# Decay matrices of a state-space scan: running sums spread by transfers instead of matmuls, work of each group's rounds moved

## The reference

```
cs[l]      = sum over k <= l of (-dt[k] * exp(a))            # the running sum of the decay
L[m, l]    = exp(cs[l] - cs[m])  if m <= l, else 0           # the decay matrix of one head
y[l]       = sum over m of (C[l] . B[m]) * L[m, l] * dt[m] * x[m]   # inside the chunk
state      = sum over m of B[m] * dt[m] * exp(cs[127] - cs[m]) * x[m]
y[l]      += exp(cs[l]) * C[l] . state                       # second chunk only
```

## Time and profile before

| | |
|---|---|
| median of three runs | 3062.14 us (3058.6 to 3064.3) |
| profiled execution | 3059.77 us, its span 3057.9 us |
| PE busy | 2883.9 us, 94% of the span |
| DVE, ACT, POOL busy | 1018.7, 566.3, 204.0 us |
| mean granted TensorE clock | 0.981 |
| traffic | 703.97 MB, 230 GB/s on the mean |
| scan of layer 0 (groups) | about 270 to 408 us |
| scan of layer 1 (groups) | about 980 to 1118 us |

### The profile page before, as it was taken

The page is one execution under the profiler, slowest core; times in us unless marked ns, Lnnn a source line. Parts: engine busy times, 40 slices in busy tenths (PEclk is TensorE's granted clock), DMA queues, the critical chain, the costliest instruction groups (busy, mean ns, idle before and its releaser), DMA issues. The chain is left out here.

```text
span 3057.9 us, 34707 instructions
## 1 busy us (share of the span) xinstructions
PE 2883.9 (94%) x14328; PEld 1697.8 (56%) x14328; DVE 1018.7 (33%) x2615; ACT 566.3 (19%) x1308; POOL 204.0 (7%) x319
## 2 busy tenths in 40 slices
PE   7999999999999999999999999999978989988986
PEld 4576646864567655884556555444444455443432
DVE  3543533421544442541435432222223064211112
ACT  1321411100231321211145110000011051000001
POOL 0000041000000000000000010000012020000001
PEclk9999999999999999999999999999989999999998
DMA  5346437454246445543040379999994125999996
GB/s 208 138 157 245 170 123 250 138 175 145 85 145 248 168 139 201 207 157 106 22 152 8 140 287 426 428 427 426 427 355 126 58 88 221 427 426 426 427 427 280
DMA packets 181448, 703.97 MB, mean 230 GB/s; under 512 B 18042, under 2 KB 27322, under 8 KB 156192
## 3 DMA queue, kind: packets, MB, share of 16 engines
q1 hardware_dynamic: 163600, 667.51, 55.9%
q0 software_dynamic: 17392, 34.11, 3.5%
q10 hardware_dynamic: 288, 0.01, 0.0%
HBM read 694.09 MB, written 20.06 MB: 234 GB/s over the span
## 5 line engine op out<-in xcount | busy, mean ns | idle before, releaser
L566 PE MATMUL bank<-h1T,wslot 128*128 128x256 f32 x2176 | 473.7, 380 | 2.2 <-issue 2.1
L566 PEld LDWEIGHTS bank<-h1T,wslot 128*128 128x128 f32 x2176 | 412.1, 190 | 61.3 <-issue 5.9
L2551 PE MATMUL bank<-wslot,xgT 128*64 128x512 f32 x736 | 337.2, 614 | 36.5 <-DMA wslot<-in_moe_w_up 18.9
L2552 PE MATMUL bank<-wslot,xgT 128*64 128x512 f32 x752 | 340.2, 608 | 0.0
L2568 DVE TENSOR_TENSOR hid<-gs,bank 64x512 f32<-64x512 f32 x65 | 68.2, 1049 | 479.8 <-ACT gs L2562 479.8
L2551 PEld LDWEIGHTS bank<-wslot,xgT 128*64 128x64 f32 x736 | 100.9, 141 | 197.1 <-issue 197.1
L2526 PEld LDWEIGHTS bank<-sel,hT 128*128 128x128 f32 x1600 | 182.8, 193 | 30.4 <-issue 25.2
L2526 PE MATMUL bank<-sel,hT 128*128 128x128 f32 x1600 | 189.0, 279 | 4.4 <-DVE sel L2505 4.4
L2606 PE MATMUL bank<-wslot,aT 128*64 128x512 f32 x736 | 164.2, 595 | 0.6 <-DVE aT L667 0.6
L2562 ACT ACTIVATE gs<-bank 64x512 f32<-64x512 f32 x65 | 38.5, 592 | 494.4 <-PE bank L2552 494.4
L451 PE MATMUL bank<-wslot,h1T 128*128 128x512 f32 (+1 forms) x320 | 121.9, 536 | 4.2 <-DVE h1T L1919 4.2
(11 more groups left out here) (415 smaller groups left out, 3882.8 us busy)
## 6 DMA issues: line engine op xcount, KB each, us to landing
wslot<-in_moe_w_up SPq DMA_DIRECT2D x47, 2048.0 KB, 20.2
wslot<-in_moe_w_gate SPq DMA_DIRECT2D x46, 2048.0 KB, 22.9
wslot<-in_moe_w_down SPq DMA_DIRECT2D x46, 2048.0 KB, 23.2
wslot<-in_w_in SPq DMA_DIRECT2D x36, 2048.0 KB, 9.0
wslot<-in_w_ada SPq DMA_DIRECT2D x24, 2048.0 KB, 8.0
wslot<-in_ffn_w_up SPq DMA_DIRECT2D x20, 2048.0 KB, 9.0
another<-in_moe_w_up SPq DMA_DIRECT2D x10, 2048.0 KB, 17.5
late<-in_moe_w_gate SPq DMA_DIRECT2D x10, 2048.0 KB, 23.1
```

The source lines that it names most:

```text
L566: ins = pe.matmul(b.t[:, 0:width], w[:, k, j * P:(j + 1) * P], xT(k), start=(k == 0), stop=(k == kc - 1))
L2551: pe.matmul(bk.t[other, :], xt.t[:, k, mine], wg[:, k, :], start=(k == 0), stop=(k == KD - 1))
L2552: ins = pe.matmul(bk.t[mine, :], xt.t[:, k, mine], wu[:, k, :], start=(k == 0), stop=(k == KD - 1))
```

## The change

The running sums of each chunk, as rows (head by token), are now made by one more matmul in `sums`, copied to SBUF and stored to DRAM. Each decay buffer is then filled by one transfer of POOL that reads the rows of 8 heads and writes them to all 128 partitions (512 KB). Four such transfers are issued when `first_ssd` begins; each of the other four of a layer when line 1535 of a chunk is emitted. The 128 matmuls of line 1495 are gone; the mask is added in place, by the same DVE instruction with SBUF as its source. Products of keys and queries, mask and Exp move from round 3 to the end of round 1; xdec is made before xs and xdt. The tile `blank` goes, its memsets use a free tile, and ACT and DVE wait for the two stores from it after the feed-forward network of layer 0.

```
+class StepSums:
+    def __init__(self, K, ctx):
+        self.K, self.n = K, 0
+        self.rows = K.sb("sumrows", [SHEADS, TT, P], ctx=ctx)
+        self.kept = self.stored = []
+    def begin(self):
+        self.dram = self.K.nc.dram_tensor(f"sum_rows{self.n}", [TT, SHEADS, P], F32).ap()
+        self.n += 1
+        self.stored = []
+    def spread(self, chunks, turn):
+        self.chunks, self.turn, self.filled = iter(chunks), turn, {}
+        for _ in turn.bufs:
+            self.fill()
+    def fill(self):
+        at = next(self.chunks, None)
+        if at is None:
+            return
+        (g, t), dc = at, self.turn.next()
+        @self.K.block.gpsimd
+        def _(p):
+            self.filled[at] = dc, self.K.move(p, dc.t[:, :, :], self.dram[t, HPG * g:HPG * (g + 1), :].partition_broadcast(P),
+                                              *dc.free, *self.stored)
...
@@ step_sizes, sums @@
             pe.matmul(b.t[:, 0:SHEADS], K.c("upto"), d(ADT), start=True, stop=True)
+            pe.matmul(b.t[0:SHEADS, P:2 * P], d(ADT), K.c("upto"), start=True, stop=True)
             K.mp = K.pe.mark(pe.matmul(b.t[:, 64:64 + SHEADS], K.c("ones"), d(ADT), start=True, stop=True).then_inc(K.pe.sem, 1))
...
+            for due in K.due(v, *S.kept):
+                v.wait_ge(*due)
+            K.mc = K.dve.mark(v.tensor_copy(S.rows[:, t, :], b.t[0:SHEADS, P:2 * P]).then_inc(K.dve.sem, 1))
+        b.free = [K.mc]
+        @K.block.gpsimd
+        def _(g):
+            S.stored.append(K.move(g, S.dram[t], S.rows[:, t, :], K.mc))
+        S.kept = S.stored
...
@@ first_ssd @@
+        S.spread([(g, t) for g in range(GROUPS) for t in range(TT)], decay)
...
+        def decays(g, t):
+            dc, came = S.filled[g, t]
+            exps = []
+            for q in range(HPG // 4):
+                @block.vector
+                def _(v):
+                    for due in K.due(v, came):
+                        v.wait_ge(*due)
+                    K.mv = K.dve.mark(v.tensor_tensor(
+                        dc.t[:, 4 * q:4 * q + 4, :], dc.t[:, 4 * q:4 * q + 4, :],
+                        K.c("segmask").unsqueeze(1).broadcast_to([P, 4, P]), ALU.add).then_inc(K.dve.sem, 1))
+                @block.scalar
+                def _(act):
+                    for due in K.due(act, K.mv, *small):
+                        act.wait_ge(*due)
+                    for i in range(4):
+                        h = HPG * g + 4 * q + i
+                        K.ml = K.act.mark(act.activation(dc.t[:, 4 * q + i, :], dc.t[:, 4 * q + i, :], ACT.Exp,
+                                                         bias=dts[:, t, NCS, h:h + 1]).then_inc(K.act.sem, 1))
+                exps.append(K.ml)
+            return dc, exps
...
                 def use(bank, mk):
+                    if t == 0:
+                        @block.vector
+                        def _(v):
+                            for due in K.due(v, mk, *small, *prev):
+                                v.wait_ge(*due)
+                            K.mv = K.dve.mark(v.tensor_tensor(hv(xdec[:, :]), hv(bank[:, :]), per_head(t, W2), ALU.mult).then_inc(K.dve.sem, 1))
+                        xm["dec"] = K.mv
...
-                    if t == 0:
-                        @block.vector
-                        def _(v):
-                            K.mv = K.dve.mark(v.tensor_tensor(hv(xdec[:, :]), hv(bank[:, :]), per_head(t, W2), ALU.mult).then_inc(K.dve.sem, 1))
-                        xm["dec"] = K.mv
                     return K.mv
                 K.transposed([xbcT[:, ch, t * P:(t + 1) * P] for ch in chs], use, *[convd[c] for c in chs], *prev)
+            multiplied = []
+            for t in range(TT):
+                b, tl = K.banks.next(), slice(t * P, (t + 1) * P)
+                @block.tensor
+                def _(pe):
+                    for due in K.due(pe, convd[16 + g], convd[20 + g], *b.free):
+                        pe.wait_ge(*due)
+                    K.mp = K.pe.mark(pe.matmul(b.t[:, 0:P], BT[:, tl], CT[:, tl], start=True, stop=True).then_inc(K.pe.sem, 1))
+                multiplied.append(K.copy(0, cbT[:, t, :], b.t[:, 0:P], K.mp, *prev))
+                b.free = [multiplied[t]]
+            grown = [decays(g, t) for t in range(TT)]
             yield
...
             def chunk(t):
                 tl = slice(t * P, (t + 1) * P)
...
-                            ins = pe.matmul(bq.t[:, i * P:(i + 1) * P],
-                                            dts[:, t, ADT, h:h + 1].broadcast_to([P, P]), K.c("upto"),
-                                            start=True, stop=True)
...
-                        K.mv = K.dve.mark(v.tensor_tensor(
-                            dc.t[:, 4 * q:4 * q + 4, :], bq.t[:, :].rearrange("p (h l) -> p h l", h=4),
-                            K.c("segmask").unsqueeze(1).broadcast_to([P, 4, P]), ALU.add).then_inc(K.dve.sem, 1))
...
+                cm = multiplied[t]
+                dc, exps = grown[t]
                 yield
...
                 dc.free = [K.mp]
+                S.fill()
...
@@ first_block, end of layer 0 @@
+            if l == 0:
+                @block.scalar
+                def _(act):
+                    for due in K.due(act, *K.blanked):
+                        act.wait_ge(*due)
+                @block.vector
+                def _(v):
+                    for due in K.due(v, *K.blanked):
+                        v.wait_ge(*due)
...
```

More of the change, by code:

```diff
@@ L1008, in turn_into_hT, with first_attention @@
     return out
-def first_attention(K, l, hT, hready, acc, gate, dts, rows_of):
+def first_attention(K, l, hT, hready, acc, gate, dts, rows_of, S):
     block = K.block
@@ L1219, in _ @@
                 gm[t] = K.act.mark(act.activation(gate[:, t, :], gate[:, t, :], ACT.Sigmoid).then_inc(K.act.sem, 1))
-        small, held.free = step_sizes(K, dts, rows_of, steps, K.second.loaded)
+        small, held.free = step_sizes(K, dts, rows_of, steps, K.second.loaded, S)
         K.banks.bufs.append(held)
@@ L1236, with step_sizes @@
 DTV, ADT, CS, NCS, ECS, W1, W2, W3 = range(8)
-def step_sizes(K, dts, rows, steps, loaded):
+class StepSums:
[20 more added lines that the diff above has]
+                                              *dc.free, *self.stored)
+def step_sizes(K, dts, rows, steps, loaded, S):
     small = []
@@ L1325, in _ @@
             K.mf = m
-        b.free = [K.mf]
+            for due in K.due(v, *S.kept):
[6 more added lines that the diff above has]
+        S.kept = S.stored
         @K.block.scalar
@@ L1343, in step_sizes, with first_ssd @@
     return small, marks
-def first_ssd(K, l, hT, hdeps, acc, cols, rows, ada, gate, spare, dts, small):
+def first_ssd(K, l, hT, hdeps, acc, cols, rows, ada, gate, spare, dts, small, S):
     block = K.block
@@ L1517, in chunk @@
+                cm = multiplied[t]
+                dc, exps = grown[t]
                 yield
-                for q, hs in enumerate(heads):
+                for q in range(HPG // 4):
                     @block.vector
@@ L1939, in first_block @@
         dts = K.sb("dts", [P, TT, 8, SHEADS], ctx=ctx)
+        sums = StepSums(K, ctx)
         rowt = second.rowt
@@ L1980, in first_block @@
                 following = second.latent_rows(diag, stat)
-            small = first_attention(K, l, hT, hready, acc, second.xc, dts, rows)
-            merged = first_ssd(K, l, hT, [*hready(0), *hready(1)], acc, cols, rows, ada, second.xc, flat[:, TT * D:], dts, small)
+            sums.begin()
+            small = first_attention(K, l, hT, hready, acc, second.xc, dts, rows, sums)
+            merged = first_ssd(K, l, hT, [*hready(0), *hready(1)], acc, cols, rows, ada, second.xc, flat[:, TT * D:], dts, small, sums)
             if l == 0:
                 spread_bias(K)
-                expert_rows(K)
+                expert_rows(K, second.xc[0:CAP, 1, :])
             first_ffn(K, l, x, hT, cols, merged, ada, following, second if l else None)
+            if l == 0:
[7 more added lines that the diff above has]
+                        v.wait_ge(*due)
         @block.vector
@@ L2321, with expert_rows @@
 SPAN_R = 2 * (SEQ // GRID_W) - 1
-def expert_rows(K):
-    K.y_dram, K.slot_rows = [], []
+def expert_rows(K, blank):
+    K.y_dram, K.slot_rows, K.blanked = [], [], []
     for l in range(2):
@@ L2334, in _ @@
         def _(v):
-            K.mv = K.dve.mark(v.memset(K.blank[:, CAP * l:CAP * l + CAP], float(rows)).then_inc(K.dve.sem, 1))
+            for due in K.due(v, (K.dve, K.dve.count)):
+                v.wait_ge(*due)
+            K.mv = K.dve.mark(v.memset(blank[:, CAP * l:CAP * l + CAP], float(rows)).then_inc(K.dve.sem, 1))
         @K.block.gpsimd
         def _(g):
-            K.blanked = K.move(g, K.slot_rows[l].rearrange("(b s) o -> b (s o)", b=CAP), K.blank[:, CAP * l:CAP * l + CAP], K.mv)
+            K.blanked.append(K.move(g, K.slot_rows[l].rearrange("(b s) o -> b (s o)", b=CAP), blank[:, CAP * l:CAP * l + CAP], K.mv))
 def spread_bias(K):
```

(3 more changed lines are left out.)

## The result

The changed kernel took **3068.4 us** (median of six runs, 3065.8 to 3074.1); the kernel before took 3060.8 us on the same chip (six runs, 3058.1 to 3064.3). The ratio is 1.0026 with a 95% interval of 1.0016 to 1.0036: slower, by 7.6 us, where 3057.4 us was forecast. The profiled execution took 3065.8 us, 3064.0 of them its span.

The account below looks back on a forecast made before the run. PE bounds the kernel, busy 94% of the span. Each of four pairs gains 3.4 - 2.0 = 1.4 us; less 0.9 for the sums, 4.7 us, so 3062.1 becomes 3057.4 us, range 3046 to 3066.

Parts of the forecast that it names:

- Path through a pair: Scan, second group's x transposes to first group's line 1535: 3.84 us shorter, with a new PE gap of 3.75 us.
- Work moved forward: First group's keys-by-queries products leave that interval for the end of its own first part: 0.44 us per pair paid earlier.
- The clock: After each pair's new PE gap the clock falls, costing 2.0 us per pair, with 0 and 3.0 as ends.
- The sums: One added two-pass matmul per chunk and layer in `sums`: 0.22 us each, 0.9 us in all.
- The transfers: Eight more 512 KB transfers per layer stay hidden under the conv stage and next group's z product: cost nothing.
- A: Rival: the clock holds after the scan's gaps, gain 12.7 us, 3049.4 us; chance 0.22 with mixtures toward it.
- B: Rival: PE does not wait at all because DVE's masks come in time, gain 27.7 us, 3034 us; chance 0.05.
- C: Rival: slower in-place DVE operations, 2.2 us more gap, clock loss 3.0: 8.1 us slower, 3070.2 us; chance 0.15 with D.
- D: Rival: transfers are not hidden, each late one costing what it is late; chance 0.15 together with C.
- The chances: Forecast odds for the total time: faster by over 0.2% 0.44, within 0.44, slower by over 0.2% 0.12.

Follow-up runs that it names:

- the filled gap: Changed kernel plus seven unread 256-column products per pair in the PE gap ahead of line 1577: 3053.4 us, ratio 0.997.
- real work in the gap: Changed kernel, second group's masks and Exps behind first group's masked products, gate's first products in the gap: 3041.0 us, ratio 0.9935; again 3042.6 us, 0.9934.
- late masks and three unread products: Changed kernel, second group's masks and Exps behind first group's masked products, three unread 128x256 products in the gap: 3042.1 us, ratio 0.9937; again 3047.8 us, 0.9948.
- transfers alone: Changed kernel with everything in its old place and order, only the running sums coming by transfer: 3070.0 us, ratio 1.0027.
- order alone: Kernel before with only the change's new order of work, matmuls of line 1495 kept, no transfers added: 3074.9 us, ratio 1.0036.
- fifteen products: Changed kernel, gap kept, fifteen unread 128x256 products between the gap and line 1577: 3088.2 us in one run.

## Why the prediction was wrong

- **Path through a pair.** 3.84 us shorter forecast, 3.87 measured; a gap of 3.75 us forecast, 3.57 measured, released by the line named. Right.
- **Work moved forward.** 0.44 us per pair forecast, 0.54 measured (352.71 to 353.25). Right.
- **The clock.** This step failed. The forecast took 2.0 us per pair, with 3.0 as the end; the runs show 4.93 and 4.41, mean 4.67, four times over: 4 x 2.67 = 10.7 us more than in the sum. Per pair, 3.87 - 0.54 - 4.67 = -1.3 us stands in place of a gain of 1.4; two pairs make 2.7 us longer, where a layer's scan grew by 2.5. The mean was drawn from eight gaps of like length elsewhere in the program, and length was the wrong thing to match them by: with wide products behind this very gap it costs 1.7 and 2.9 us, mean 2.3, which is nearly what the eight had said (2.0; the granted clock inside the gaps, 0.84 over the 3.35 us up to 2797.60 and 0.88 over the 3.16 us up to 59.79, gives 0.5 and 0.4 us where 0.5 to 0.8 was read, and makes it 2.1). Directly behind this gap stand 16 products of 64 columns, 32 records 0.11 us apart from start to start. The trace of the kernel before could have told that the eight are of another kind. Behind two of the eight gaps stand four short records and then products of 256 columns, behind five of them 512 columns, behind one 128. The products behind the first and the last gap of the earlier trace rows's four:

```profile
772.50 4.48 PE L1120 MATMUL bank<-kiT,qiT 64*128 64x256 f32 x24
...
2797.60 1.09 PE L2551 MATMUL bank<-wslot,xgT 128*64 128x512 f32 x1 [3.35 <-DMA wslot<-in_moe_w_up]
```

- **The sums.** 0.22 us forecast for each of four added matmuls, 0.45 measured; 1.8 us instead of 0.9. From start to start the products of `sums` stood 0.14 to 0.23 us apart before. Now the added one (line 1347) holds PE for 0.33 or 0.34 us, and the ones around it stand 0.24 to 0.31 us apart: line 1481's 0.22 us was too low for the product itself, and its effect on its neighbours was not in the sum.
- **The transfers.** Forecast free, and they are: no DVE wait on one in the scan, and DVE's line 1464, in place on a tile that a transfer wrote, keeps its 0.60 us.
- **Rivals.** A, the clock holds: not here, but the filled gap is its case, 3053.4 us beside the 3049.4 worked out. B, no wait at all: real work in the gap comes nearest, 0.9935. C gave 3070.2 us, near what came, but by luck, for its mechanism isn't there: DVE's operations are no longer than before. Its size was that of a lost clock of 3.0 us and a longer gap; the clock alone did it. D did not happen.
- **The chances.** 0.12 for slower was too little: the bound of 3.0 us for the clock was the worst of eight cases, none of which had 64-column products behind it, so it was no bound. For faster the parts that are named add up to 0.46, not 0.44.

## What to carry to other kernels

When products are taken out of a path that DVE nearly fills, work out the gap that is left, and then price it with the granted clock *and* the products that run right behind it: here a gap of 3.57 us ahead of 64-column products cost 4.7 us more in clock, more than it was long, and even gaps of 1.61 us cost 3.4 or 5.1 in seven pairs of eight, and nothing in the eighth. Close such a gap before judging the change: first reorder DVE so that what PE waits for comes first, then pull independent products into what is left. With that, the same change went from 1.0026 to 0.9935 of the time before; three products per pair that nobody reads were worth 16 to 19 us by the ratios (1.0000 to 0.9948 and 0.9937).

## What the runs showed of the hardware that was not expected

The same gap does not always lower the clock. Behind the scan PE waits 1.91 us for xbcT in both layers, ahead of the same products. In the kernel before, the clock held in both. In the kernel with late masks and three unread products, layer 0 and then layer 1 (columns as above):

```profile
395.99:439.19 43.20, 43.20 (x101) 19.27 (x102) 4.15 (x6) 0.00 (x0) 8.11 (x16) 1.00 0.44 153
1096.24:1139.44 43.20, 43.20 (x97) 19.10 (x98) 2.79 (x5) 0.00 (x0) 0.00 (x0) 0.96 0.38 138
```

Layer 1 falls to 0.96, which is 1.7 us of work, in both profiles of this kernel and in both of the one with real work in the gap. It falls there too in layer 0 of the kernel with transfers alone and in both layers of the one with fifteen products. The pairs of transfers alone (clock 0.69 and 1.00 behind one gap of 1.73 us) and of the order alone (0.77 and 1.00 behind 1.61 us) show the same. The Trainium skill, "TensorE: Matmul & The Clock Gate", section "What's actually happening", says that the chip watches PE's activity on a schedule that runs freely and is not restarted with the kernel, so that the same products meet it at different points. The two layers and the two pairs agree with that. It would also let one kernel differ from execution to execution. In the scans there is little of that: the changed one took 140.09 to 140.30 us in four layers of two profiles. (The kernel before, 137.61 us each time, loses no clock there and so can't tell.) Outside them there is. These are the two profiles of late masks with unread products, from behind layer 1's scan to the end:

```profile
1096.24:3041.70 1945.46, 1805.49 (x8972) 987.54 (x8972) 563.33 (x1338) 311.77 (x705) 134.21 (x188) 0.97 0.66 264
1099.02:3041.00 1941.98, 1797.31 (x8972) 982.25 (x8972) 563.61 (x1338) 311.45 (x705) 134.15 (x188) 0.98 0.66 265
```

The same 8972 records keep PE busy 8.2 us longer in one than in the other, at a lower clock. A difference of a few us between two kernels, read from one profile of each, is therefore no evidence outside the scans.
